# A hybrid decoder step on one core: how x comes in, the projection's order, and the attention's tile order, sums and gathers

## The reference

```
u = rms_norm(h, g_pre);  p = u @ w_in            # 1088 rows, 24 tiles of 128 columns and the gates
A: for 8 query heads over 2 kv heads, three branches, each a masked softmax attention:
   compressed blocks of 32 keys, selected blocks of 64 keys (top 16), window of 512 keys;
   their outputs are mixed with sigmoid gates
B: GLU -> causal conv (31 taps) -> group norm -> swish -> pointwise
C: causal conv (4 taps) -> gates -> linear recurrence
h = h + rms_norm(concat(A, B, C) * silu gates @ w_out, g_post)
```

## Time and profile before

| | us |
|---|---|
| median of 3 runs | 977.46 (976.9 to 978.73) |
| the profiled execution, its own time | 977.14 |
| its span in the profile | 975.3 |
| PE / DVE / ACT / POOL busy | 901.2 / 598.5 / 372.3 / 105.9 |
| granted PE clock, mean | 0.975 |

### The profile page before, as it was taken

The page is one execution under the profiler, slowest core; times in us unless marked ns, Lnnn a source line. Parts: engine busy times, 40 slices in busy tenths (PEclk is TensorE's granted clock), DMA queues, the critical chain, the costliest instruction groups (busy, mean ns, idle before and its releaser), DMA issues.

```text
span 975.3 us, 16013 instructions
## 1 busy us (share of the span) xinstructions
PE 901.2 (92%) x6261; PEld 573.8 (59%) x6261; DVE 598.5 (61%) x1136; ACT 372.3 (38%) x846; POOL 105.9 (11%) x104
## 2 busy tenths in 40 slices
PE   3999999999899998998899999998786999999997
PEld 2565666566456665766576876776553666544443
DVE  4378888999987895976366657666742444322222
ACT  4211243310012201034876877766633566411111
POOL 1011110000010111100102111221141321000000
PEclk9999999999999999999999999999987999999999
DMA  8332561422043355452800000000028789632111
GB/s 302 149 130 107 162 242 31 69 59 85 23 149 142 111 203 195 150 204 76 289 2 1 2 2 1 2 2 1 1 82 329 272 313 344 242 119 87 65 54 54
DMA packets 32110, 118.34 MB, mean 121 GB/s; under 512 B 3433, under 2 KB 11771, under 8 KB 22971
## 3 DMA queue, kind: packets, MB, share of 16 engines
q0 software_dynamic: 9360, 68.16, 19.2%
q1 hardware_dynamic: 19053, 43.39, 12.7%
q10 hardware_dynamic: 3623, 5.76, 2.8%
HBM read 108.33 MB, written 13.29 MB: 125 GB/s over the span
## 4 chain that ended last, share of the span: by engine, by line
PE 60%; DVE 20%; DVEq 6%; issue 4%; ACT 3%; DMA 3%; SPq 2%; POOL 1%; ACTq 1%; POOLq 0%
PE PS L838 13%; PE PS L2024 11%; DVE main L649 8%; PE PS L1573 6%; PE PS L1563 5%; PE PS L1591 4%; PE PS L811 3%; PE PS L1875 3%; PE PS L1854 3%; DVE main L611 3%; PE PS L1886 2%; PE PS L1541 2%; PE PS L1909 2%; DVE main L608 2%; ACT main L1383 2%
## 5 line engine op out<-in xcount | busy, mean ns | idle before, releaser
L838 PE MATMUL PS<-main 128*128 128x352 f32 (+1 forms) x1056 | 331.2, 473 | 0.0
L838 PEld LDWEIGHTS PS<-main 128*128 128x128 f32 x1056 | 202.2, 192 | 121.2 <-issue 4.8
L1383 ACT ACTIVATE main<-PS,main 128x512 f32<-128x512 f32 (+3 forms) x192 | 104.0, 562 | 45.9 <-DVE main L1412 21.5
L2024 PE MATMUL PS<-main 128*128 128x512 f32 x256 | 112.3, 593 | 0.1
L434 ACT ACTIVATE main<-PS 128x384 f32<-128x384 f32 x24 | 11.8, 490 | 219.1 <-PE PS L838 210.6
L649 DVE SCALAR_TENSOR_TENSOR main<-main,par 128x1022 f32<-128x1022 f32 (+16 forms) x66 | 83.8, 1270 | 5.3 <-issue 0.4
L1573 PE MATMUL PS<-cst,main 128*128 128x128 f32 x528 | 73.8, 288 | 8.8 <-ACT main L1383 8.7
L608 DVE TENSOR_TENSOR main<-main 128x1024 f32<-128x1024 f32 x64 | 75.4, 1220 | 9.8 <-DMA main<-in_cmp_k_dram,row 5.3
L2024 PEld LDWEIGHTS PS<-main 128*128 128x128 f32 x256 | 47.6, 190 | 56.4 <-issue 56.4
L611 DVE TENSOR_TENSOR main<-main 128x1024 f32<-128x1024 f32 (+2 forms) x96 | 75.0, 781 | 7.2
L1375 ACT ACTIVATE main<-PS 128x512 f32<-128x512 f32 (+1 forms) x138 | 69.7, 597 | 18.8 <-PE PS L1573 18.6
(11 more groups left out here) (316 smaller groups left out, 1040.8 us busy)
## 6 DMA issues: line engine op xcount, KB each, us to landing
main<-in_w_tiles_dram SPq DMA_DIRECT2D x24, 512.0 KB, 3.7
out_dram<-main SPq DMA_DIRECT2D x18, 256.0 KB, 2.1
main<-in_x_prompt_dram SPq DMA_DIRECT2D x8, 512.0 KB, 10.2
main<-in_w_out_dram SPq DMA_DIRECT2D x4, 1024.0 KB, 6.2
main<-in_x_prompt_dram SPq DMA_DIRECT2D x16, 256.0 KB, 3.0
out_dram<-main SPq DMA_DIRECT2D x4, 512.0 KB
diag<-in_win_k_dram SPq DMA_DIRECT2D x8, 256.0 KB, 7.6
diag<-in_win_v_dram SPq DMA_DIRECT2D x8, 256.0 KB, 8.2
```

The source lines that it names most:

```text
L838: last = pe.matmul(bank(3 * s + j)[:, 0:w], ring[:, s, k * P:(k + 1) * P], xT[:, k, t0:t0 + w], start=(k == 0), stop=(k == KD - 1))
L1383: last = act.activation(prob[:, k % 2, g, h * nk_ * P:(h + 1) * nk_ * P], score_set(k, g)[:, h * nk_ * P:(h + 1) * nk_ * P], ACT.Exp, scal ...
L2024: last = pe.matmul(out_bank(m, h), proj[:, MIX[k], n * P:(n + 1) * P], wo[:, k, h * 512:(h + 1) * 512], start=(x == 0), stop=(x == KD - 1))
```

## The change

1. **x's way in.** ACT puts the epsilon in the root itself (`bias`), so DVE's `square` is gone; an early root loads the table once. ACT issues the loads of `rel_bias` later, those of the parameters first. DVE's tables come after the startup. PE turns half tiles inside the chunks, and a chunk's first four matmuls wait for the first half alone.
2. **Projection's order.** Pair 6 is whole ahead of the first means; means and variances lie between the chunks of pair 7. DVE takes two compress steps out of the stretch before the pointwise products and puts them behind. `pe_decode_keys` comes after the first chunk of pair 10.
3. **Way into the attention.** Three sets of banks for the natural layout, two of nine copies by DVE; SiLUs in groups of three and one, the last behind the prompt turn.
4. **Pairs.** The tile order is 7, 0, 6, 1, 5, 2, 4, 3; tiles 0 to 3 get buffers of their own. DVE peaks the first step of a batch at the end of the batch before and the second behind the first slot of side work. Steps with 4 heads (7 of 69) have their sums made by DVE (`row_sums`) instead of by ACT. No side is left for the decode loop.
5. **Gathers.** Round 0's values are gathered behind the keys of round 1, half by half.

```diff
 def act_startup(act):
-    (5 loads of rel_bias, pages, parameters)
+    act.dma_start(par[:, :], dram["parameters"]).then_inc(ld_par, 16)
+    act.dma_start(pages[:, :], dram["pages"]).then_inc(ld_pg, 16)
+    act.wait_ge(pads_done, 1)
+    act.activation(late[:, 1:2], eps, ACT.Sqrt)
...
-                if n >= 1:
-                    root(n - 1)
+                act.wait_ge(sq_done, n + 1)
+                act.activation(rstd[0:rows, n:n + 1], ssq[0:rows, n:n + 1], ACT.Sqrt, scale=1.0 / D, bias=eps[0:rows, :]).then_inc(rms, 1)
 def dve_startup(dve):
+            scale(0)
+            dve.wait_ge(ld_par, 16)
+            for n in range(9):
+                evac(n, 0)
+                if n < 8:
+                    scale(n + 1)
+                evac(n, 1)
+                if n == 3:
+                    dve_rows(dve)
+            dve_tables(dve)
 def pe_startup(pe):
+            for n in range(3):
+                turn(n, 0)
+                turn(n, 1)
+            chunk(0, 0, {1: (3, 0), 3: (3, 1), 5: (4, 0)})
+            chunk(1, 0, {1: (4, 1), 3: (5, 0), 5: (5, 1)})
+            chunk(0, 1, {1: (6, 0), 3: (6, 1), 5: (7, 0)})
+            chunk(1, 1, {1: (7, 1), 3: (8, 0), 5: (8, 1)})
+            chunk(0, 2, {})
+            chunk(1, 2, {})
...
+        ORDER = [7, 0, 6, 1, 5, 2, 4, 3]
...
             def exp(k):
+                if k - 2 in SUMMED:
+                    act.wait_ge(SEM["row_sum"], SUMMED.index(k - 2) + 1)
...
+                        if heads == R:
+                            last = act.activation(prob[...], score_set(k, g)[...], ACT.Exp, scale=-1.0, bias=peaks_of(i)[:, u:u + 1])
+                            continue
+            def row_sums(k):
+                dve.wait_ge(SEM["p_sb"], 2 * k + 2)
+                for g in range(G):
+                    last = dve.tensor_reduce(sums_of(i)[...], prob[:, k % 2, g, :].rearrange("p (h n) -> p h n", h=R), X, ALU.add)
+                last.then_inc(SEM["row_sum"], 1)
+                dve.drain()
 the loop of dve_pairs:
+            peak(BATCH[0][0])
             for b in range(TAIL + 1):
+                for j in range(2):
+                    (part_out and side of slot j, for batch b - 1)
+                    if j == 0:
+                        for k in batch(b)[1:]:
+                            peak(k)
+                        (gaps of a tile done in b)
+                for k in batch(b):
+                    if k in SUMMED:
+                        row_sums(k)
                 (weights of a tile done in b)
-                for k in batch(b + 1):
+                for k in batch(b + 1)[:1]:
                     peak(k)
 def pool_decode(pool):
-            for h in range(2):
-                pool_values(pool, 0, h)
             for rnd in range(4):
                 for h in range(2):
                     if rnd < 3:
                         pool.wait_ge(SEM["kused"], 2 * rnd + h + 1)
                         pool_keys(pool, rnd + 1, h)
                     if rnd >= 1:
                         pool.wait_ge(SEM["vused"], 2 * (rnd - 1) + h + 1)
-                        pool_values(pool, rnd, h)
+                    pool_values(pool, rnd, h)
 order on DVE:
+            dve_mean(dve, 0, 2)
             dve_compress(dve, 12, 13)
-            dve_mean(dve, 0, 2)
...
-            dve_compress(dve, 16, 20)
+            dve_compress(dve, 16, 18)
 order on PE:
-            pe_project(pe, 6, 0, 4)
+            pe_project(pe, 6)
             pe_mean(pe, 0, 2)
-            pe_project(pe, 6, 4, 5)
-            pe_mean(pe, 2, 4)
-            pe_project(pe, 6, 5, 6)
-            pe_mean(pe, 4, 6)
+            for q in range(2):
+                pe_project(pe, 7, q, q + 1)
+                pe_mean(pe, 2 * q + 2, 2 * q + 4)
             for q in range(3):
-                pe_project(pe, 7, q, q + 1)
+                pe_project(pe, 7, q + 2, q + 3)
                 pe_var(pe, 2 * q, 2 * q + 2)
...
+            pe_project(pe, 10, 0, 1)
             pe_decode_keys(pe)
-            pe_project(pe, 10, 0, 1)
```

More of the change, by code:

```diff
@@ L941, in program @@
         vct = carve(a1 + 7888, P)
-        assert a1 + 8272 <= FREE
+        wgt_s, peaks_s, sums_s = [carve(a1 + 8272 + 16 * n, 16) for n in range(3)]
+        oraw_s = late[:, 0:2 * 512].rearrange("p (c n) -> p c n", c=2)
+        oo_s = late[:, 2 * 512:3 * 512]
+        assert a1 + 8320 <= FREE
         sc = carve(at["proj"], 2048)
@@ L1010, in pe_natural, with natural, nat_bank, natural_free @@
                 last.then_inc(SEM["nat_ps"], 1)
-        def act_natural(act):
-            for n in range(9):
-                w = P if n < NT else S
-                act.wait_ge(SEM["nat_ps"], n + 1)
-                o, i = nat[0:w, :, n, :], bank(2 * (n % 2), 2)[0:w, 0:6 * P].rearrange("p (s c) -> p s c", s=6)
-                act.activation(o, i, ACT.Copy).then_inc(SEM["nat_sb"], 1)
+        NAT_DVE = [5, 7]
+        def natural(eng, copy, mine):
+            for j, n in enumerate(mine):
+                w = P if n < NT else S
+                eng.wait_ge(SEM["nat_ps"], n + 1)
+                o, i = nat[0:w, :, n, :], nat_bank(n)[0:w, 0:6 * P].rearrange("p (s c) -> p s c", s=6)
+                copy(o, i).then_inc(nat_sb[n in NAT_DVE], 1)
+        def nat_bank(n):
+            return bank(2 * (n % 3), 2)
+        def natural_free(eng, n):
+            by_dve = n in NAT_DVE
+            eng.wait_ge(nat_sb[by_dve], sum((x in NAT_DVE) == by_dve for x in range(n + 1)))
+        def act_natural(act):
+            natural(act, lambda o, i: act.activation(o, i, ACT.Copy), [n for n in range(9) if n not in NAT_DVE])
+        def dve_natural(dve):
+            natural(dve, dve.tensor_copy, NAT_DVE)
         def wait_natural(eng):
-            eng.wait_ge(SEM["nat_sb"], 9)
+            eng.wait_ge(nat_sb[0], 9 - len(NAT_DVE))
+            eng.wait_ge(nat_sb[1], len(NAT_DVE))
         def sp_natural(sp):
@@ L1281, in program, with before, raw, mixed @@
         STEPS, TILE_STEPS, TILE_PARTS, PARTS = [], {}, {}, []
-        ORDER = list(range(NT - 1, -1, -1))
+        ORDER = [7, 0, 6, 1, 5, 2, 4, 3]
+        def before(i):
+            same = [n for n, x in enumerate(ORDER) if n < ORDER.index(i) and ((x < 4 and i < 4) or (x >= 4 and i >= 4 and x % 2 == i % 2))]
+            return max(same, default=-1) + 1
+        def raw(i, c):
+            return oraw_s[:, c, :] if i < 4 else oraw[:, i % 2, c, :]
+        def mixed(i):
+            return oo_s if i < 4 else oo[:, i % 2, :]
+        def peaks_of(i):
+            return peaks_s if i < 4 else peaks_p[:, i % 2, :]
+        def sums_of(i):
+            return sums_s if i < 4 else sums[:, i % 2, :]
+        def weights_of(i):
+            return wgt_s if i < 4 else wgt
         for i in ORDER:
@@ L1301, in program @@
         LAST_PART = {i: max(n for n, p in enumerate(PARTS) if p[0] == i) for i in ORDER}
+        SUMMED = [k for k in range(NS) if STEPS[k][7] == R]
         def width(k):
@@ L1456, in weights @@
                 if i >= 4:
+                    pk, gp, w, top = views(i)
                     dve.wait_ge(SEM["stat_exp"], 8 - i)
```

195 lines of the change are left out of this document (85 added, 110 removed).

## The result

The changed kernel takes **951.2 us** (median of 4 runs, 949.57 to 952.55) beside 977.18 of the kernel before on the same chip: a ratio of 0.9738, 95% interval 0.972 to 0.9756. The forecast was 948 with 936 to 960. The profiled execution took 949.57 us, its span is 947.4, so 27.9 us of span are gone.

A forecast was written before the change was run, and what follows sets the result against it. The prediction took PE's fixed-order stream to bound the kernel, gains coming only from its waits and half clock. Terms summed to -30.9 us, cut to -29.5 for small stops: 948 us, range 936 to 960.

The forecast's parts named there:

- rival of a late x: Startup: x lands late, so part 1 gives only 5 us; 953 us in total, 8% chance.
- rival that DVE holds the front back: Projection to masks: compress steps pile up, PE waits at the masks, +9 instead of +1.3; 958 us, 17% chance.
- price that I had put on DVE: Projection: DVE stands some 5 us at its first mean and starts normalising only 6 us earlier.
- The 2.7 us of the earlier trace: Way into the attention: PE's wait for ACT's copy goes as SiLUs no longer sit before it, -2.7 us.
- The last term: Start of attention: last SiLU and exp table load cover the first peak, first exp 0.7 us late, +0.6.
- (a): Pairs: second peak behind the first side costs 0.85 us in each of five one-side batches, +4.2 us.
- (b): Pairs: DVE's row sums and light batches following each other, less ACT's saving, cost net +4.5 us.
- (c): Pairs: a batch with two-head peaks ahead of a side's product goes from 11.98 to 9.05 us, -2.9.
- The tail: End of the pairs: tile 3 there instead of tile 0 gains another 1.1 us.
- rival that the pairs gain as well: Pairs: the new order is shorter and DVE's sums hide, part 4 becomes -6; 937 us, 20% chance.
- The half clock behind the wait: Decode, behind the wait for round 1's keys: half clock goes over some 4 us of work, -2.8 us.
- The other side: Pairs: the second peak behind the first side costs every batch, 1.1 us each; 982 us, 3% chance.

The follow-up runs named there:

- e5: The kernel before with part 1 of the change alone: 965.04 us, ratio 0.9884.
- e6: The kernel before with parts 1 and 2 of the change: 949.66 us, ratio 0.9729.
- e7: The changed kernel with part 4's work order undone: old tile order, both peaks early, sums by ACT, DVE's `gaps` behind the peaks; 942.04 us.
- e1: The changed kernel with both halves of round 0's values gathered ahead of the keys of round 1 again: 957.21 us, ratio 0.9812.
- e9: The kernel of e8 with DVE copying tiles 6 and 8 of the natural layout instead of 5 and 7: 934.28 us, ratio 0.9584.
- e8: The changed kernel with ACT's sums, second peak late only where two-head steps meet two sides, otherwise both early, `gaps` behind the peaks: 934.12 us.
- e3: The changed kernel with both peaks of a batch at the end of the batch before, and DVE's `gaps` behind the peaks: 940.81 us, ratio 0.965.
- e11: The kernel of e8 with tiles in the order 7 down to 0: 940.38 us, ratio 0.9646.

## Why the prediction was right, and where its terms were not

The total held because errors stood against each other. Measured run against run, parts 1 and 2 gave 8.5 us more than forecast (27.4 for 18.9), part 4 cost 4.5 more (9.2 for 4.7), and parts 3 and 5 together gave 9.1 less (7.6 for 16.7). That this comes out 3.5 us from the forecast is in good part luck. By its own steps:

| step | forecast | measured |
|---|---|---|
| part 1 | -10.5 | -12.0 (e5), first pair ended 12.2 earlier there, 11.3 in the kernel after |
| part 2 | -8.4 | -15.4 (e6 against e5), 9.4 of it ahead of the first scores |
| part 3 | -2.6 | -1.3 to the first scores (e7 against e6), inside the 3 us of chance there; the first exp 0.6 late |
| part 4 | +4.7 | +9.2 (after against e7) |
| part 5 | -14.1 | -6.0 in the changed kernel (e1); with part 3 and old tiles -7.6 (e7 against e6), 10.7 in the trace |
| sum | -30.9, forecast -29.5 | -26.0 |

**Part 1** went as laid out: first turn at 7.85 (7.8), tile 5 squared at 22.45 (22.5), the first chunk at 15.40 instead of 14.3. A tile took DVE and PE 2.8 us, not 2.3, since PE turned at half clock (1.97 for 8 turns) and DVE stood 0.61 us for it. The rival of a late x is out: behind the first tile ACT waits for x 0.76 us at one tile and 2.05 at another, and PE has none of it.

**Part 2.** No PE wait at the means, 1.56 us at the masks, as said (1.3). But DVE stood only 1.95 us at the first mean, not 5, and it normalises from 286.72, 11.7 us earlier than in the earlier trace rows instead of 6. DVE's timeline:

```profile
254.29 1.22 DVE L724 TENSOR_TENSOR main<-main,PS 128x384 f32<-128x384 f32 x2 [1.95 <-PE PS L872]
...
286.72 2.55 DVE L741 RECIPROCAL main<-main 128x384 f32<-128x384 f32 x1 [0.64 <-ACT main L506]
```

The rival that DVE holds the front back is out. The price that I had put on DVE was too high: ahead of the first scores part 2 gave 9.4 us for the 8.4. Most of the error is elsewhere, the 3.9 us behind the first scores in e6, mostly clock (another 2.1 lie between spans and medians). They were no term at all, and one trace of each kernel does not show that they belong to part 2.

**Part 3.** The 2.7 us of the earlier trace rows were counted as part 3's, but part 2 makes another wait right ahead of it and takes it along (e6). The copies of DVE bring a wait of 1.77 that I had not seen; e9 shows that it only moves, and e8 that it is not always there. The last term held: the first exp is some 0.6 us late, behind the SiLU and the table (the first batch takes 5.99 us instead of 5.42), ACT's timeline:

```profile
445.60 1.11 ACT L1145 ACTIVATE main<-main 128x1088 f32<-128x1088 f32 x1
446.79 1.28 ACT L1429 ACT_TABLE_LOAD   x1
...
448.09 0.69 ACT L1429 ACTIVATE main<-PS,main 128x512 f32<-128x512 f32 x1
```

The Trainium skill ("ScalarE: Activation LUTs", What ACT_TABLE_LOAD costs) adds 1.38 us of drain to each switch. Here the load starts 0.08 us behind the SiLU, and the exp 0.01 us behind the load; the trace does not show such a drain.

**Part 4** is the step that failed. (a) The late peak: "five batches have one side: +4.2". The 0.82 a batch was right (7.40 against 6.58), the count was not, because I had taken "with two sides PE needs 7.6 anyway" over to batches of 3 keys and light ones, where PE is not that long. Measured: 11.0 us in the trace where it costs, in 13 batches; 8.3 with what it gives in the others, 10.4 by the medians (e3). (b) The row sums: +4.5, measured 4.9 to 5.7 by the medians, of which the batches of the traces have 2.3 to 3.2. The reduce takes 680 ns:

```profile
L1478 DVE TENSOR_REDUCE main<-main 128x4 f32<-128x512 f32 x14 | 9.0, 680 | 0.5
```

So the 0.69 of the earlier trace rows held. The 62 cycles less that the Trainium skill ("VectorE: DVE Perf Modes", The TRN2 errata) gives for a source in SBUF, which made my estimate of 0.6, do not show. (c) The late peak's gain, -2.9 for a batch of two-head steps, was taken from the one such batch of before, 11.98 us long, of which 1.6 is half clock (as in e5); at full clock it takes 10.33, so the late peak gives 1.3 there (9.07). The tail gained more than the 1.1 I gave it, since tile 0's sides also held the keys back (e1). The rival that the pairs gain as well is out for this kernel and came true in e8: without the row sums and with the peaks mixed, part 4 is worth -7.9 (942.0 to 934.1).

**Part 5.** No wait for the keys, as said, and none for round 0's values. From the last side to the first keys of round 1 it is 18.2 us (702.42 to 720.62, forecast 17.6). But the gathers and the tile order shorten the same stretch, and what one is worth depends on the other. From the last scores to the end the gathers give 10.7 us with the old tiles (275.1 in e6, 264.4 in e7) and 6.4 with the mixed order (263.5 in e1, 257.1); the mixed order gives 11.6 with the old gathers (e6, e1) and 7.3 with the new (e7, after). Both together give 18.0 (e6, after), not the 22.3 of each by itself. (These pairs differ in the other work of parts 3 and 4 too, nearly all of which lies ahead of the last scores.) The step that failed is this overlap: with -14.1 I gave part 5 what two parts did together, and counted tile 0's sides in part 4 as nothing more than their matmuls. The half clock behind the wait was worth 0.6 us and not 2.8: from the first keys to the end it is 227.4 in e1 and 226.8 after.

The other side (a late peak that costs every batch) is out: the batches of 4 keys without sides stayed at 5.71, except the first (5.99 in both) and the one behind tile 4's light batch (6.83, in e3 5.88). Its mechanism was the right one to fear: in 13 batches it took 11 us.

## What to carry to other kernels

Where an in-order engine has two kinds of work, ask of each piece who waits for it: the product that frees a bank may stand ahead of the peak only in batches where PE needs that bank sooner than the exp. Count such batches by what bounds each, not by one case measured: even the rule of e8 takes in one batch too many. And test a change of five parts by its parts: two of them gave all of its gain here, and one, put right, gave 17 us more.

## What the runs showed of the hardware

- A reduce of 128x512 floats took 680 ns from SBUF and 0.69 us from PSUM.
- Four exps of 128x128 without a sum took 1.14 us together in the kernel after, started 0.25 us apart. With a sum, in e8, they start 0.34 to 0.36 apart; the sum's read is a record of its own of 0.19 us and more, about half of which lies under the next exp.
- The activation table took 1.28 us at each of its 14 loads in the kernel after, with 0.01 us to the instruction behind it where that waited for nothing.
- PE's granted clock over the batches fell from 0.99 to 0.97 with the longer waits, and e8 had 0.99 again: in the light batches a wait was paid twice, in us and in half clock (scores of 3 keys 2.93 instead of 1.56 us).
- The length of a wait did not settle the clock behind it: behind 3.07 us the same 16 turns took 3.56 us in e5 and 1.97 in e6, and behind 1.77 us for DVE's copy the prompt turn took 3.40 in the kernel after, and behind 1.76 us 1.94 in e11.
- Gathers of 1 MB issued behind 4 MB of others (e1) were used 15.1 us behind their issue, after a wait; with nothing ahead 11.9 us sufficed without one (708.77 to 720.62).
